# A compressor's products over neighbouring blocks: three in place of four in half of its slices

## The reference, cut to what matters

```python
def compress_blocks(kv, pos_emb, w1, w2):
    per = CMP_LEN // CMP_STRIDE                       # 32 // 16 = 2
    n_cmp = (t - CMP_LEN) // CMP_STRIDE + 1
    pieces = kv[:, :CMP_STRIDE * (n_cmp + per - 1)].reshape(n, n_cmp + per - 1, CMP_STRIDE, g, hd)
    blocks = jnp.concatenate([pieces[:, j:j + n_cmp] for j in range(per)], axis=2)
    hid = jax.nn.silu(jnp.einsum('nilgd,ldf->nigf', blocks + pos_emb[None, None, :, None, :],
                                 w1.reshape(CMP_LEN, hd, CMP_HIDDEN)))
    return jnp.einsum('nigf,fd->nigd', hid, w2)
```

## Time and profile before

| | us |
|---|---|
| median of 3 executions (1786.83 to 1790.98) | 1787.87 |
| the profiled execution, first to last instruction | 1786.0 |
| the stage of the change, first to last product of L3229 | 267.5 |
| from there to the last result of the stage | 12.5 |

### The profile page before, as it was taken

The page is one execution under the profiler, slowest core; times in us unless marked ns, Lnnn a source line. Parts: engine busy times, 40 slices in busy tenths (PEclk is TensorE's granted clock), DMA queues, the critical chain, the costliest instruction groups (busy, mean ns, idle before and its releaser), DMA issues. The chain is left out here.

```text
span 1786.0 us, 34260 instructions
## 1 busy us (share of the span) xinstructions
PE 1725.0 (97%) x13111; PEld 1412.2 (79%) x13111; DVE 892.8 (50%) x2673; ACT 695.8 (39%) x1535; POOL 418.0 (23%) x591
## 2 busy tenths in 40 slices
PE   7999999999899899999999999999799999999998
PEld 5878778678776778887789787787688888888998
DVE  5322222288456445222224555454677787778534
ACT  4200000176332323100112334233687877787413
POOL 0000000000464000000003342331365656565300
PEclk9999999999999999999999999999899999999999
DMA  5443343464889765466434442536400000000154
GB/s 211 147 171 135 141 152 111 148 225 138 258 259 287 258 227 193 116 196 206 135 98 157 161 140 92 196 110 165 119 20 25 26 26 24 22 14 8 59 163 156
DMA packets 148409, 245.31 MB, mean 137 GB/s; under 512 B 34939, under 2 KB 82808, under 8 KB 145944
## 3 DMA queue, kind: packets, MB, share of 16 engines
q1 hardware_dynamic: 132936, 198.48, 34.4%
q0 software_dynamic: 7424, 33.56, 5.5%
q10 hardware_dynamic: 7888, 11.08, 2.1%
HBM read 201.35 MB, written 48.77 MB: 140 GB/s over the span
## 5 line engine op out<-in xcount | busy, mean ns | idle before, releaser
L1998 POOL TENSOR_SCALAR sparse_pr<-sparse_pr,sparse_coef,sparse_gate 128x63 f32<-128x63 f32 (+8 forms) x384 | 247.1, 662 | 160.8 <-DVE sparse_coef L1938 160.8
L1884 ACT ACTIVATE sparse_pr<-sparse_pr,sparse_nmax 128x63 f32<-128x63 f32 (+8 forms) x384 | 227.7, 595 | 67.5 <-DVE sparse_nmax L1932 67.3
L1246 PE MATMUL x_acc<-x_w_hi,x_y_lo 128*128 128x512 f32 (+3 forms) x448 | 157.3, 351 | 1.6 <-DVE x_y_lo L1058 1.4
L1246 PE MATMUL x_acc<-x_w_lo,x_y_hi 128*128 128x512 f32 (+3 forms) x448 | 155.3, 347 | 0.0
L1246 PE MATMUL x_acc<-x_w_hi,x_y_hi 128*128 128x512 f32 (+3 forms) x448 | 154.9, 346 | 0.0
L511 PE MATMUL h_acc<-h_w_hi,h_y_lo 128*128 128x512 f32 x384 | 151.7, 395 | 0.8 <-DVE h_y_lo L433 0.8
L511 PE MATMUL h_acc<-h_w_lo,h_y_hi 128*128 128x512 f32 x384 | 150.1, 391 | 0.0
L511 PE MATMUL h_acc<-h_w_hi,h_y_hi 128*128 128x512 f32 x384 | 149.9, 390 | 0.0
L1805 PE MATMUL sparse_ps<-cmp_lent,ss_pieces 64*128 64x384 f32 (+3 forms) x928 | 136.6, 421 | 5.2 <-DVE sparse_part L1932 3.5
L1817 PE MATMUL sparse_ps<-constants_shared,sparse_pr 128*128 128x128 f32 x1120 | 132.9, 276 | 3.3 <-DVE sparse_nmax L1932 2.2
L458 DVE COPY cmp_w<-h_acc 128x512 f32<-128x512 f32 x48 | 33.2, 691 | 204.6 <-PE h_acc L511 204.6
(11 more groups left out here) (406 smaller groups left out, 3474.0 us busy)
## 6 DMA issues: line engine op xcount, KB each, us to landing
h_w_side<-in_even_w_in SPq DMA_DIRECT2D x16, 896.0 KB
h<-cmp_w SPq DMA_DIRECT2D x48, 256.0 KB, 2.0
h_w_raw<-in_even_w_in SPq DMA_DIRECT2D x6, 2048.0 KB, 8.9
x_w_side<-in_odd_w_in SPq DMA_DIRECT2D x16, 716.0 KB, 6.7
cmp_lent<-in_odd_w_in SPq DMA_DIRECT2D x5, 2048.0 KB, 9.3
ev_unit<-in_cache_a_k SPq DMA_DIRECT2D x4, 2048.0 KB
ev_unit<-in_cache_a_v SPq DMA_DIRECT2D x4, 2048.0 KB
h_turned<-x_out SPq DMA_DIRECT2D x32, 256.0 KB, 2.7
```

The costliest lines, as they stand in the source:

```text
L1246: last = nc.tensor.matmul(acc[b][:, 0:passes[p][3]], left[:, k, t * P:(t + 1) * P], weights(right, p)[:, k, :], start=(k == 0 and a == 0), ...
L1884: nc.scalar.activation(row, row, ACT.Exp, scale=-1.0, bias=nmax[u % UB][:, e * NBR + br:e * NBR + br + 1], accum_out=lsum[u % UB][:, e * N ...
L1998: nc.gpsimd.tensor_scalar(row, row, one, gate[:, t, 2 * i + e, (br + 1) % 3:(br + 1) % 3 + 1], ALU.mult, ALU.mult).then_inc(scaled, 1)
```

## The change

Pieces are split into even and odd ones: `turn_x` writes 256 even columns (E) and 256 odd columns (O) of a step apart. Even blocks need W0·E + W1·O, odd blocks W0·O + W1·E', with E' the even pieces one further on. In the slices 0, 1, 6 and 7 these four products are made as they stand. In the slices 2 to 5 (`SHARED`) three take their place: (W0+W1)·O in a bank of its own (`ps_x`), W0·(E−O) in the even columns and W1·(E'−O) in the odd ones. Every product is three matmuls of 256 columns. GpSimd makes the two differences of a step in one instruction (`differ`). At an item's end ACT copies `ps_x` to SBUF (`take_both`), DVE adds it to both kinds of block (`add_parts`), and ACT's Silu reads the sum.

With it comes another order: all four items of keys (n = 0 to 3), then the four of values. Only one set of weights is held; the values' weights are loaded again in a ring of three tiles (`w_next`), summed on POOL, cast on ACT and subtracted on DVE during item 3. The rest of the attention of pair p lies in the items e = 2p and o = 2p + 1, by a table of events; the compressed values' product comes separately, four items after. The block-score table `overlap` follows the new order of blocks. ACT takes all copies of turned keys, half of which were DVE's. Scores go through one bank in place of two.

```diff
-    c, b = np.arange(NCS)[:, None], np.arange(NSL)[None, :]
+    c = np.concatenate([np.arange(0, NCS, 2), np.arange(1, NCS, 2)])[:, None]
...
+    SHARED = (2, 3, 4, 5)
...
+        tail = (o, 11) if p == 0 else (o, 8)
...
+        at(*later(0), "mask", p)
+        at(*later(1), "exp", p)
+        at(*later(2), "coef", p)
+        at(*later(3), "scale", p)
+        for x in range(2):
+            turn_at(*later(6), "psel", p, x)
+            turn_at(*later(7), "psel", p, 2 + x)
+        turn_at(*later(8), "pwin", p, 0)
+        turn_at(*later(8), "pnew", p, 0)
+        at(*later(10), "values", p)
+        at(*later(11), "acc", p)
+    for p in range(PAIRS):
+        at(p + 1, 1, "down_k", p)
+        at(PAIRS + p + 1, 1, "down_v", p)
+        at(PAIRS + p + 1, 4, "cmp_values", p)
+        at(PAIRS + p + 1, 4, "out", p)
...
+    def step_ahead(n, hh):
+        t = n * KD + hh // 2 + AHEAD
+        return t if hh % 2 == 0 and t < N_STEPS else None
...
+        def differ(eng, t):
+            eng.wait_ge(x_turned, t + 1)
...
+            raw = x_raw[t % 2][:, :]
+            after = bass.AP(tensor=raw.tensor, offset=raw.offset, ap=[raw.ap[0], [1, 2], [1, XP]])
+            odd = raw[:, XO_AT:XO_AT + XP].unsqueeze(1).broadcast_to([P, 2, XP])
+            nc.gpsimd.tensor_tensor(raw[:, E_AT:E_AT + 2 * XP].rearrange("p (r c) -> p r c", r=2), after, odd, ALU.subtract).then_inc(x_diff, 1)
...
+        def take_x_high(act, t):
+            f, l = divmod(t, KD)
+            if shared(l):
+                act.wait_ge(x_diff, f * len(SHARED) + sum_at(l) + 1)
+            else:
+                act.wait_ge(x_turned, t + 1)
...
+            if t >= N_X:
+                act.wait_ge(x_used, t - N_X + 1)
+            nc.scalar.copy(x_part(x_hi, t), raw_part(t)).then_inc(x_high, 1)
...
+                for n, hh in slots():
+                    t = step_ahead(n, hh)
+                    if t is not None and t + 1 < N_STEPS and shared((t + 1) % KD):
+                        differ(pool, t + 1)
+                    if n == 0 and hh < 4:
+                        for x in (2 * hh, 2 * hh + 1):
+                            gather_quarter(pool, 1, x)
+                    if hh >= 7 and hh < 15 and n + 2 < ITEMS:
+                        gather_quarter(pool, n + 2, hh - 7)
+                    if n == PAIRS - 1 and hh >= 2 and hh % 2 == 0 and shared(hh // 2 - 1):
+                        next_sum(hh // 2 - 1)
+                    for what, p, *x in events(n, hh):
...
+                        if what == "scale":
+                            pool.wait_ge(coef_ready, p + 1)
...
+                    def product(to, wh, wl, at, start=False, stop=False):
+                        for i, (w, x) in enumerate(((wh, x_lo), (wl, x_hi), (wh, x_hi))):
+                            last = nc.tensor.matmul(to, w, x[b][:, at:at + XP], start=start and i == 0, stop=stop and i == 2)
+                        return last
...
+                        pe.wait_ge(x_cut, t + 1)
+                    if first:
+                        if n:
+                            pe.wait_ge(summed, 2 * n - 1 + second)
...
+                    if not shared(l):
+                        even, odd = ps_h[second][:, 0:XP], ps_h[second][:, XP:2 * XP]
+                        product(even, *half(0, second), 0, start=first)
+                        product(even, *half(1, second), XO_AT)
+                        product(odd, *half(0, second), XO_AT)
+                        last = product(odd, *half(1, second), 1, stop=final)
...
+                    if not second:
...
+                        for c in range(2):
+                            last = product(ps_x[:, c * XP:(c + 1) * XP], *both_halves(c), 0, start=l == SHARED[0] and c == 0, stop=l == SHARED[-1] and c == 1)
...
+                        product(ps_h[0][:, 0:XP], *half(0, 0), XP)
+                    else:
+                        product(ps_h[0][:, XP:2 * XP], *half(1, 0), 2 * XP)
+                        product(ps_h[1][:, 0:XP], *half(0, 1), XP)
+                        product(ps_h[1][:, XP:2 * XP], *half(1, 1), 2 * XP).then_inc(x_used, 1)
...
+                def take_both(n):
+                    act.wait_ge(both_done, n + 1)
...
+                    nc.scalar.copy(both_sb[:, :], ps_x[:, :]).then_inc(both_taken, 1)
...
+                def next_high_part(l):
+                    act.wait_ge(next_in[l % RING_W], 64 * (l // RING_W + 1))
+                    act.wait_ge(x_used, (PAIRS - 1) * KD + l + 1)
+                    last = nc.scalar.copy(w_hi[:, l, :, :], w_next[l % RING_W][:, :, :])
...
+                def add_parts(n, c):
+                    if c == 0:
+                        dve.wait_ge(hidden_done, n + 1)
+                    else:
+                        dve.wait_ge(x_used, (n + 1) * KD)
...
+                    dve.wait_ge(both_taken, n + 1)
...
+                    nc.vector.tensor_tensor(to, own, both, ALU.add).then_inc(summed, 1)
...
+                def other_work(n, hh):
+                    if hh == HALVES - 1 and n < ITEMS:
+                        add_parts(n, 0)
+                    if hh == 0 and n:
+                        add_parts(n - 1, 1)
+                    for what, p, x in turns_of(n, hh):
+                        if not by_act(what, x):
+                            take(dve, what, p, x)
+                    if n < ITEMS and step_ahead(n, hh) is not None:
+                        take_x_low(dve, step_ahead(n, hh))
+                    if (n, hh) == (PAIRS, 1) or n == PAIRS - 1 and hh >= 3 and hh % 2 == 1:
+                        next_low_part(KD - 1 if n == PAIRS else (hh - 3) // 2)
```

More of the change, by code:

```diff
@@ new lines, in attend_samples_sparse, with at, turn_at, later @@
+    N_STEPS = ITEMS * KD
+    N_PC = 3
+    SHARED = (2, 3, 4, 5)
+    RING_W = 3
+    turns_at, events_at = {}, {}
+    def at(n, hh, what, *x):
+        events_at.setdefault((n, hh), []).append((what, *x))
+    def turn_at(n, hh, what, p, x):
+        turns_at.setdefault((n, hh), []).append((what, p, x))
+    for p in range(PAIRS):
+        e, o = 2 * p, 2 * p + 1
+        for a in range(2):
+            turn_at(e, 5 + a, "win", p, a)
+        for q in range(8):
+            turn_at(*((e, 11 + q) if q < 5 else (o, q - 5)), "ks", p, q)
+        turn_at(e, 15, "new", p, 0)
+        cmp_item, c0 = (o, 3) if p == 0 else (e, 4)
+        at(cmp_item, c0, "cmp", p)
+        at(cmp_item, c0 + 1, "norm", p)
+        turn_at(cmp_item, c0 + 5, "pc", p, 0)
+        at(cmp_item, c0 + 6, "share", p)
+        at(cmp_item, c0 + 7, "sum", p)
+        at(o, 5, "new", p)
+        for x in range(5):
+            at(o, 3 + x, "scores", p, x)
+        tail = (o, 11) if p == 0 else (o, 8)
+        def later(k):
+            n, hh = tail[0], tail[1] + k
+            return n + hh // HALVES, hh % HALVES
+        at(*later(0), "mask", p)
[9 more added lines that the diff above has]
+        at(*later(11), "acc", p)
@@ L2986, in attend_samples_sparse @@
         xT_p, p_turned = comp.xT_p, comp.p_turned
-        hid_p = [hid[m][:, :, 0, :, 0:NCB] for m in range(2)]
+        hid_p = [hid[:, :, m, :, 0:NCB] for m in range(2)]
         kc_p, vc_p = pn[:, 0:NCB], o_cmp[0:NCB, :]
@@ L3060, in take @@
                     eng.wait_ge(av_done, p)
-                if what == "pc":
-                    last = copy(pcT[:, :], src[0:NCS, 0:R2])
-                elif what == "psel":
+                if what == "psel":
                     last = copy(pselT[:, 4 * x:4 * x + 4, :], src[:, :].rearrange("p (c k) -> p c k", c=4))
@@ new lines, in scores_new @@
+                def scores_new(p):
+                    copied("new", p, 0)
+                    if p == 0:
+                        pe.wait_ge(cmp_probs, 1)
+                    elif p == 1:
+                        pe.wait_ge(kc_ready, 3)
+                    else:
+                        pe.wait_ge(vc_ready, 2 * p - 3)
+                    for a in range(2):
+                        half = slice(a * 64, a * 64 + 64)
+                        last = nc.tensor.matmul(ps_m[half, M_NEW], q_all[:, 2 * p + a, :], newT[:, a, :, :].rearrange("p x j -> p (x j)"),
+                                                start=True, stop=True)
+                    last.then_inc(new_scored, 1)
@@ L3258, in down_k @@
-                def down_k(p):
-                    pe.wait_ge(active, hidden_count(0, p, 1))
-                    if p:
-                        pe.wait_ge(vc_ready, p)
+                    if 5 * p + x:
+                        pe.wait_ge(s_free, 5 * p + x)
+                    for a in range(2):
+                        half, lhs = slice(a * 64, a * 64 + 64), q_all[:, 2 * p + a, :]
+                        rhs = ksT[a][:, x * 512:(x + 1) * 512] if x < 4 else kwT[a]
+                        last = nc.tensor.matmul(ps_s[half, :], lhs, rhs, start=True, stop=True)
@@ L3371, in take_v, with silu @@
+                def silu(n, c):
+                    act.wait_ge(summed, 2 * n + c + 1)
```

(8 more changed lines are left out.)

668 lines of the change are left out of this document (356 added, 312 removed).

## The result

The changed kernel takes 1811.49 us (median of 4 runs, 1808.67 to 1814.24) against 1787.76 of the kernel before on the same chip: ratio 1.0135, 95% interval 1.0117 to 1.0152. Slower by 24 us (1.35%); the forecast was 1782, and its range ended at 1797. Read first are the page's busy times and granted clock, as in the earlier trace rows.

A forecast was written before the change was run, and what follows sets the result against it. PE was taken to set the pace. Products -18.3, handoffs +0.8, item-end queues +12, start +0.6 and end -0.8 gave -5.7 us on a 1786.0 us span, 1780.3; the median lies 1.87 above, so 1782 us, range 1766 to 1797.

The forecast's parts named there:

- The products: Compressor matmuls on PE: 1344 of 256 columns at 0.1205 us replace 768 of 512 columns, -18.3 us.
- Rival C: A load not hidden under short matmuls: about 0.134 us each, nothing gained, 1800 us with the stalls; chance 0.08.
- The queues at an item's end: PE waits behind mask, scaling, difference and subtraction in odd items, none in even ones: +12 us, bounds 0 and 30.
- Contention: GpSimd's differences slow DVE's subtractions: up to 32 x 0.5 = 16 us of DVE lost, which fit on average.
- Rival B: DVE's addition is late at every item's end, eight times 3.7 us: 1800 us; chance 0.14.
- item 1's gathers: Gathers moved behind two differences on POOL: hidden by eight slots, otherwise up to 3.7 us.
- The weight ring: Values' weights reloaded: hides behind items 0 to 3; as rival D it stalls item 4, +5, 1787 us; chance 0.11.
- the turns behind the scaling: PE reaches the turned probabilities of pairs 1 to 3 before they are ready: a stall of 1.1 us each.
- the start: One more DVE subtraction ahead of the queries' copy delays PE's first product: +0.6 us, at most 1.4.
- Handoffs: PE switching between products and other work: 8 more handoffs over four pairs, about 0.1 us each, +0.8 us.
- The end: After the last product: two turns now lie before it, one copy added, the chain of vc off: -0.8 us.

The follow-up runs named there:

- e2: Changed kernel with the differences made by VectorE instead of GpSimd: 1817.87 us, ratio 1.0152 to the kernel before.
- e1: Changed kernel with GpSimd's difference covering 8 of 256 columns, the rest left out: 1809.24 us, ratio 1.0100 to the kernel before.
- e6: Changed kernel, at an item's end DVE adds before it subtracts and ACT casts before it copies: 1803.28 us, ratio 1.0081 to the kernel before.
- e13: Kernel before with gathers of 64 numbers in place of 512 from the third item on: 1787.43 us, ratio 1.0000.
- e5: Kernel before with each product of 512 columns made as two of 256, in all slices: 1811.71 us, ratio 1.0136.
- e14: Kernel before with all products split as in e5, and gathers of 64 numbers from the third item on: 1794.15 us, ratio 1.0037.
- e7: Changed kernel with slices 3 to 6 shared and the summed weights' subtraction moved before the first slice: 1810.86 us, ratio 1.0118 to the kernel before.
- e18: e12 with slices 3 to 6 shared in place of 2 to 5, and gathers of 64 numbers from the third item on: 1800.64 us, ratio 1.0069.
- e9: Changed kernel with products of 512 columns in slices 0, 1, 6 and 7, 960 matmuls: 1812.93 us, ratio 1.0137 to the kernel before.
- e12: e11 with products of 512 columns in slices 0, 1, 6 and 7: 1800.55 us, ratio 1.0078 to the kernel before.
- e11: Changed kernel with e6's two reorderings, the summed weights' subtraction before the first slice and one values' weight cast later: 1803.47 us, ratio 1.0099.

## Why the prediction was wrong

The forecast had the stage at 262 us, and it took 287.8. Of these 26 us, queues that hold PE up at the items' ends and before the turned probabilities are 6 (17.9 us measured, 12 forecast), waits that it put at nothing 9, the half clock that it did not have 8.5, and handoffs with what was not told apart 6.5; the products gave 2 us more than forecast, and 2.9 us of such waits stood in the kernel before already.

**The products.** Predicted 0.1205 us each, measured 0.119, 1344 of them: right, -20 in place of -18.3. (The forecast's own factors, 0.117 by 1.035, give 0.121, an error of under 1 us.) By the load rule of the Trainium skill (TensorE: Matmul & The Clock Gate, Part 3, "The mechanism"), which I set aside, each would have cost some 214 ns; the trace disagrees with it at 256 columns as well. Rival C (0.134) is out.

**The queues at an item's end: the step that failed.** I put +12 us on them, "in even items DVE has nothing in that place: none". The odd ends came near in sum: 4.0 + 1.34 + 2.72 = 8.1 us measured, 2.2 + 2 x 3.7 + 0.5 = 10.1 forecast. That is luck in part, since end by end it was 4.0 against 2.2, 1.34 against 4.2 and 2.72 against 3.7. The even ones came out at 1.15 + 2.32 + 2.36 + 0.90 = 6.7 us in place of none. The end of item 4, in after's timeline on three engines:

```profile
1160.42 0.59 ACT L3114 COPY cmp_lent<-ss_ps_t 128x512 f32<-128x512 f32 x1 [1.27 <-PE ss_ps_t L3297]
...
1160.90 0.84 ACT L3175 CAST ss_x_hi<-ss_x_raw 128x768 fp32r<-128x768 f32 x1
...
1161.77 2.42 DVE L3181 TENSOR_TENSOR ss_x_lo<-ss_x_raw,ss_x_hi 128x768 fp32r<-128x768 f32 x1 [2.03 <-ACT ss_x_hi L3175]
1162.10 1.27 POOL L3145 TENSOR_TENSOR ss_x_raw<-ss_x_raw 128x512 f32<-128x512 f32 x1
...
1164.11 0.68 DVE L3656 TENSOR_TENSOR ss_hid<-ss_ps_h,ss_both 128x512 f32<-128x512 f32 x1
...
1164.93 0.36 PE L3334 MATMUL ss_ps_h<-ss_x_lo,ss_w_hi 128*128 128x256 f32 x1 [2.36 <-DVE ss_hid L3656]
```

No mask and no scaling is near. ACT, which now takes all copies of turned keys, takes one ahead of the cast; DVE, idle 2.03 us for the cast, then needs 2.42 us beside GpSimd for a subtraction that takes 0.96 alone (e2's mean), and the addition stands behind it. I had counted the copies as ACT's load and not as a place in its queue. Contention I had priced on average, up to 0.5 us in each of 32 steps. It is not spread so: in the changed kernel 26 of the 32 subtractions of 768 columns take 0.93 to 0.97 us, some of them beside a difference, and six take 1.26 to 3.58 us. Two of the six stand right before an addition, at the ends of items 2 and 4, whose waits are 2.32 and 2.36 us; with the short differences of e1 both subtractions take 0.96 us and both waits 0.90. So at the even ends some 0.9 us each come from the place in the queue, and 1.4 us at two of them from GpSimd. The longest of the six stands beside GpSimd's scaling, behind the end of item 1:

```profile
1049.64 3.58 DVE L3181 TENSOR_TENSOR ss_x_lo<-ss_x_raw,ss_x_hi 128x768 fp32r<-128x768 f32 x1 [0.81 <-ACT ss_x_hi L3175]
```

Rival B had the right side and place, DVE's addition late at every end, with 14.8 us where it had 29.6; its 1800 is not the 1811 either. e6 shows the place: turning these two queues round takes 10.8 us of these waits away and 8 us off the time. (By the Trainium skill, GPSIMD Engine Reference, "Key points", the two engines share SBUF interfaces; the 2.42 against 0.96 agrees.)

**The other waits** are 9 us that the sum put at nothing. I gave nothing to item 1's gathers ("those eight slots hide them"), but PE waits 2.8 us for ACT's copy, since ACT stands at the cast of an item-1 slice that has not come; DVE waits for the gather before it turns the slice:

```profile
1001.79 1.06 DVE L3156 STREAM_TRANSPOSE ss_x_raw<-ss_pieces 128x256 f32<-128x256 f32 x2 [4.69 <-DMA ss_pieces<-in_cache_c_kcmp,cmp_quarters]
1002.88 0.62 ACT L3175 CAST ss_x_hi<-ss_x_raw 128x520 fp32r<-128x520 f32 x1 [5.65 <-DVE ss_x_raw L3156]
```

The weight ring was a rival of +5 at item 4; it cost 4.6 us at another place: ACT's cast of a weight slice waits for GpSimd's sum, queued behind the scaling, and the copy of turned probabilities behind that cast:

```profile
1122.23 0.73 POOL L3239 TENSOR_TENSOR ss_w_next_sum<-ss_w_next 128x256 f32<-128x256 f32 x1
1122.99 0.40 ACT L3551 CAST ss_ws_hi<-ss_w_next_sum 128x256 fp32r<-128x256 f32 x1 [6.06 <-POOL ss_w_next_sum L3239]
1123.30 0.58 ACT L3131 COPY cmp_w<-ss_ps_t 128x512 f32<-128x512 f32 x1
```

At the turns behind the scaling I had 1.1 us each for pairs 1 to 3; measured 1.54 and 1.53 for two. At the start the products begin 0.6 us later, the number forecast, but that can't be told from chance: the kernel before starts its stage at 978.10 in its profile and at 982.24 in e13, which is the same up to there. The first shared slice waits 1.6 us more.

**The clock, a term that the sum lacked.** Before, products ran at 1.2 GHz at the start alone; after, in six stretches behind waits, which makes about +8.5 us. I had priced a wait at its own length. Handoffs were put at +0.8 us; with what was not told apart they are 7.

**The end** was forecast 0.8 us shorter and became 0.5 longer. Two loads on engines off the critical path were too low in the text as well: a difference took 1.49 us where I took 1.25, and doubling the cost of all 128 transposes would have been +54 us and not +27.

**What stays open.** Why e5's signals of PE come late. In the old order it takes short products and gather traffic together (e5, e13, e14). But the changed kernel has both and shows none in its profile, while e1, e6 and e7, with as many short products and the same traffic, show some, and in the new order thin gathers don't remove them (e18). With one profile each it can't be told whether a small shift of the order decides this or chance. Whether the recording of so many instructions has a part in it can't be told: all runs were recorded. Also, how much of the changed kernel's loss comes from its short products cannot be split off: widening half of them gave nothing with the waits in place (e9 against the changed kernel) and 0.2% with the ends mended (e12 against e11), within the intervals.

## What to carry to other kernels

Before a tuned order of queues is rewritten for an eighth fewer columns, list for each new instruction what stands behind it on its engine, copies included, at every item's end, and price PE's waits with the half clock behind them. Test the new tile width alone, in the old order, first: the split of the kernel before was one line and would have told that the gain was at risk. Where two engines slow each other down, look for the place where the slow one stands right before what the bounding engine waits for; the mean hides it. Where an engine's wait has no working engine before it in the profile, compare the start of its instruction with the end of the one that signals it.

## What the runs showed of the hardware that was not expected

- A signal of PE reached DVE 4.6 us after the end of the matmul that gives it (e5, 1052.74 to 1057.64), and 0.04 us after it with an eighth of the gathered bytes (e14).
- Matmuls of 256 fp32r columns with a load each start every 0.119 us, half of 0.235 at 512; reading the two halves of a product of 512 columns in reversed order (e9) needs no longer.
- A DVE transpose with a strided output took 628 ns in place of 420; the subtraction of 768 columns 956 ns with no difference on GpSimd (e2). With the differences there the mean is 1182 ns, but 26 of 32 still take 0.93 to 0.97 us and the other six 1.26 to 3.58 (the changed kernel).
- GpSimd's difference with 512 columns of output took 1487 ns in the mean and with 16 columns 432 ns (e1).
- Behind waits of 1.3 to 4.6 us PE's products ran at 1.2 GHz for 3 us and more in six places of the changed kernel; behind one of 2.36 us they stayed at 2.4 GHz.
